# Eight key pages before the stream, a kept raw memory, and samples' outputs ahead of the diagonals in a two-layer decoder step

## The reference, cut to what matters

```python
def memory_kv(mem, g_mem, w_mem):                       # once for each layer
    k, v = jnp.split(rmsnorm(mem, g_mem) @ w_mem, 2, axis=-1)
def fox_layer(...):                                     # layer 0
    q, k, v, f, q_mem, gate = jnp.split(rmsnorm(x, g_pre) @ w_in, FOX_SPLITS, axis=-1)
    logf = log_sigmoid(f + b_f)
    o_tok = attend(q, k, v, logf)    # samples: k_pool[page_table], v_pool[page_table], decays
    o_mem = memory_attend(q_mem, mem_k, mem_v)
    y = (concat(o_tok, o_mem) * silu(gate)) @ w_o
    return x + rmsnorm(y, g_post)
def wkv_recurrence(...):                                # layer 1, per token
    sa = einsum('bhvk,bhk->bhv', S, -kk_t)
    S = S * w_t + sa[..., None] * (kk_t * a_t) + v_t[..., None] * k_t
    y_t = einsum('bhvk,bhk->bhv', S, r_t)
```

## Time and profile before

| | us |
|---|---|
| median of 3 runs | 1873.95 (1868.57 to 1874.59) |
| the profiled execution | 1869.83 |
| its span | 1868.1 |
| work outside the span | 1.7 |
| TensorE busy, weight loads busy | 1704.2, 1301.7 |
| VectorE busy | 964.6 |
| ScalarE busy | 378.3 |
| GpSimd busy | 161.2 |
| HBM traffic over the span | 226 GB/s |

### The profile page before, as it was taken

The page is one execution under the profiler, slowest core; times in us unless marked ns, Lnnn a source line. Parts: engine busy times, 40 slices in busy tenths (PEclk is TensorE's granted clock), DMA queues, the critical chain, the costliest instruction groups (busy, mean ns, idle before and its releaser), DMA issues.

```text
span 1868.1 us, 25962 instructions
## 1 busy us (share of the span) xinstructions
PE 1704.2 (91%) x8786; PEld 1301.7 (70%) x8786; DVE 964.6 (52%) x4842; ACT 378.3 (20%) x954; POOL 161.2 (9%) x295
## 2 busy tenths in 40 slices
PE   8999978898889998989979989999999998899996
PEld 6867755566566666657867767777777776678885
DVE  4346757655565655422352467776777776431103
ACT  2010112111121111211110323333333333121101
POOL 0001212122112222110000000000000000020000
PEclk9999989999989999999999999999999998999998
DMA  9239999999999999974353222222222214364331
GB/s 363 98 127 411 396 421 368 415 414 419 417 350 420 418 419 417 354 274 180 141 191 135 83 94 94 94 94 94 94 94 94 94 27 152 102 237 174 135 136 47
DMA packets 103637, 424.31 MB, mean 227 GB/s; under 512 B 42028, under 2 KB 48080, under 8 KB 93776
## 3 DMA queue, kind: packets, MB, share of 16 engines
q0 software_dynamic: 41680, 218.91, 29.4%
q1 hardware_dynamic: 53400, 189.64, 27.1%
q10 hardware_dynamic: 8424, 14.10, 2.0%
HBM read 409.74 MB, written 12.87 MB: 226 GB/s over the span
## 4 chain that ended last, share of the span: by engine, by line
PE 59%; DMA 23%; DVE 11%; issue 3%; SPq 2%; ACT 1%; POOLq 1%; POOL 0%; ACTq 0%; DVEq 0%
PE psum L683 12%; PE psum L631 10%; PE psum L620 10%; DMA kvr<-in_cv 9%; DMA kvr<-in_ck 9%; PE psum L983 7%; PE psum L857 3%; DVE kvr L1730 2%; SPq L512 2%; DVE kmT L2085 2%; PE psum L669 2%; DVE kmT L2083 2%; DMA kmT<-solved_t 1%; PE psum L1051 1%; PE psum L1069 1%
## 5 line engine op out<-in xcount | busy, mean ns | idle before, releaser
L1730 DVE CUSTOM_DVE_ANT_0 kvr<-kvr,arena 128x128 f32<-128x128 f32 x1536 | 334.5, 285 | 162.7 <-DMA kvr<-in_ck 162.6
L631 PE MATMUL psum<-hT,wring 128*128 128x264 f32 x1408 | 346.7, 402 | 0.0
L631 PEld LDWEIGHTS psum<-hT,wring 128*128 128x128 f32 x1408 | 270.6, 197 | 81.3 <-issue 31.0
L983 PE MATMUL psum<-hT,kvr 128*128 128x264 f32 x1152 | 292.7, 402 | 0.0
L983 PEld LDWEIGHTS psum<-hT,kvr 128*128 128x128 f32 x1152 | 221.4, 198 | 44.8 <-issue 6.4
L857 PE MATMUL psum<-kvr,arena 128*32 128x384 f32 x1024 | 116.0, 527 | 43.0 <-DMA kvr<-in_cv 40.0
L683 PE MATMUL psum<-hT,kvr 128*128 128x264 f32 x512 | 124.6, 400 | 1.3 <-DMA kvr<-in_wg 1.3
L1730 DVE DVE_READ_ACCUMULATOR2_ANT arena<- 128x1 f32 x1536 | 123.3, 80 | 0.0
L631 PE MATMUL psum<-gT,wring 128*128 128x256 f32 x512 | 120.1, 391 | 0.0
L620 PE MATMUL psum<-gT,wring 128*128 128x264 f32 x512 | 115.9, 390 | 0.8 <-DVE gT L1950 0.8
L631 PEld LDWEIGHTS psum<-gT,wring 128*128 128x128 f32 x512 | 97.8, 195 | 24.3 <-issue 10.7
(11 more groups left out here) (384 smaller groups left out, 1981.0 us busy)
## 6 DMA issues: line engine op xcount, KB each, us to landing
kvr<-in_ck POOLq DMA_DIRECT2D x128, 768.0 KB, 13.1
kvr<-in_cv POOLq DMA_DIRECT2D x128, 768.0 KB, 14.2
kvr<-in_wrkv SPq DMA_DIRECT2D x12, 3072.0 KB, 14.8
wring<-in_wkv SPq DMA_DIRECT2D x12, 2048.0 KB, 11.6
wring<-in_wm SPq DMA_DIRECT2D x8, 2048.0 KB, 12.0
wring<-in_wg SPq DMA_DIRECT2D x8, 2048.0 KB, 11.7
wring<-in_wo SPq DMA_DIRECT2D x8, 2048.0 KB, 8.2
kvr<-in_wg SPq DMA_DIRECT2D x8, 2048.0 KB, 9.8
```

Source lines behind the costliest of these rows:

```text
L631: last = mm(psum[:, m % 2, 0:n], w[:, k, t * P:(t + 1) * P], rhs[:, k, 0:n], start=(k == 0), stop=(k == KT - 1))
L983: last = mm(psum[:, m % 2, 0:T], w[:, k, t * P:(t + 1) * P], hT[:, k, :], start=(k == 0), stop=(k == KT - 1))
L1730: last = v_.tensor_tensor_reduce(page, page, qb[:, n % 2, h * P:(h + 1) * P], 1.0, 0.0, ALU.mult, ALU.add, S[:, n % 2, j * FH + h:j * FH + ...
```

## The change

1. **Eight key pages early.** `FIRST = KRING + VRING`: pages 0 to 3 go to the key ring and pages 4 to 7 to the value ring, all issued without a wait. The first four value pages are issued at slots 12, 14, 16 and 18. The scores of these eight pages are made in three chunks of four heads (`first_scores`), two of them on VectorE inside the prologue, the third in slots 0 to 7. To that end TensorE and ACT spread query chunks 0 and 1 inside the prologue (after units 2 and 4); chunk 2 stays where all three stood.
2. **The memory.** `memv` stays raw; layer 0's normed copy goes to `memv0` (in `oT`), and its 16 scaling instructions move from the prologue to slot 4 of VectorE's stream. The second load of the memory and its wait are gone.
3. **The plan.** Slots 0 to 7 weigh 0.4, slots 8 to 18 0.85, later ones 1.0 when the steps are spread.
4. **The turn.** On VectorE `diagonals()` moves behind the samples' outputs and the `prepared` increment.

```diff
--- before.py
+++ after.py
@@ -129,7 +129,9 @@
 NK = KST[-1]
 
 V_OVER = NK - KRING
-K_FILLS, V_FILLS = NK // KRING + 1, NK // VRING - 1
+K_FILLS, V_FILLS = NK // KRING, NK // VRING
+
+FIRST = KRING + VRING
 
 LAG = 3
 VSLOT = []
@@ -139,7 +141,7 @@
 SLOTS = VSLOT[-1] + 1
 V_AT = {slot: n for n, slot in enumerate(VSLOT)}
 
-V_EARLY = {6 + 3 * n: n for n in range(VRING)}
+V_EARLY = {FIRST + KRING + 2 * n: n for n in range(VRING)}
 STREAM_OF = [n for n in range(N_STREAMS) for _ in range(NPG[n])]
 
 NCH = [NS if x == MS else FH // 4 for x in STREAMS]
@@ -183,10 +185,13 @@
 
 def steps_of_slots():
 
+
+    weight = [0.4 if n < FIRST else 0.85 if n < VSLOT[0] else 1.0 for n in range(LAST_FILL)]
+    ends = [sum(weight[:n + 1]) / sum(weight) for n in range(LAST_FILL)]
     out, spent = [[] for _ in range(SLOTS)], 0.0
     for x in STEPS0:
         for part in [(*x, n) for n in range(4)] if x[0] == "unit" else [x]:
-            out[min(int(spent / TOTAL0 * LAST_FILL), SLOTS - 1)].append(part)
+            out[min(sum(e <= spent / TOTAL0 + 1e-9 for e in ends), SLOTS - 1)].append(part)
             spent += COST[x[0]] / (4 if x[0] == "unit" else 1)
     return out
 
@@ -403,6 +408,8 @@
         gmem = lambda l: gvec[:, 2, l, :]
         memv = gflat[:, 0:KT * NMEM].rearrange("p (k t) -> p k t", k=KT)
 
+        memv0 = oT[:, :, 0:NMEM]
+
         def val(i, per, k):
 
             return k if i is None else i * per + k
@@ -468,10 +475,6 @@
                     sp.dma_start(muL[:, :], I["muL"]).then_inc(sem("vec_in2"), 16)
                     sp.dma_start(lnv[:, :, :].rearrange("p a b -> p (a b)"), I["lnv"]).then_inc(sem("vec_in2"), 16)
                     sp.dma_start(shL[:, :, :], I["shL"]).then_inc(sem("vec_in2"), 16)
-                if (kind, first) == ("k", 0):
-
-                    sp.wait_ge(sem("p_done"), M_OF["m0", 7] + 1)
-                    sp.dma_start(gflat[:, 0:KT * NMEM], I["memT"].rearrange("p k t -> p (k t)")).then_inc(sem("mem_in2"), 16)
                 if (kind, first) == ("wo", 2):
 
                     sp.wait_ge(sem("u_out"), 1)
@@ -575,9 +578,10 @@
             for slot in range(SLOTS):
                 if slot < NK:
                     i = STREAM_OF[slot]
-                    if slot >= KRING:
-                        pool.wait_ge(sem("k_used"), slot - KRING + 1)
-                    page("k", kring, "k_full", slot, STREAMS[i], slot - KST[i])
+                    if slot >= FIRST:
+                        pool.wait_ge(sem("k_used"), slot - (FIRST if slot < FIRST + KRING else KRING) + 1)
+                    ring, full = (vring, "v_full") if KRING <= slot < FIRST else (kring, "k_full")
+                    page("k", ring, full, slot, STREAMS[i], slot - KST[i])
                 if slot in V_EARLY:
                     n = V_EARLY[slot]
                     page("v", vring, "v_full", n, STREAMS[STREAM_OF[n]], n - KST[STREAM_OF[n]])
@@ -768,7 +772,7 @@
                     if kind in ("m0", "m1"):
                         if at[1] == 0:
                             pe.wait_ge(sem("n_out"), 1 if kind == "m0" else 2)
-                        half_tile(m, half, memv, NMEM)
+                        half_tile(m, half, memv0 if kind == "m0" else memv, NMEM)
                     else:
                         half_tile(m, half, hT, T)
                 elif name == "f":
@@ -806,8 +810,10 @@
             def spread_queries(n, c):
                 x, nth = STREAMS[n], CST[n] + c
                 pe.wait_ge(sem("qb_c"), nth)
-                if nth == 0:
-                    pe.wait_ge(sem("lf_d"), 3)
+                if nth < 2:
+                    pe.wait_ge(sem("p_free"), M_OF["q", 4 * c + 3] + 1 + 2)
+                if nth:
+                    pe.wait_ge(*((sem("lf_c"), 1) if nth == 1 else (sem("lf_d"), 3)))
                 if x == MS and c == 0:
                     pe.wait_ge(sem("p_free"), M_OF["qm", 3] + 1 + 2)
                 for h in range(4):
@@ -836,7 +842,7 @@
                 x, j = STREAMS[n], v - KST[n]
                 ring = vring if v < V_OVER else kring
                 if v < V_OVER:
-                    pe.wait_ge(sem(f"v_full{v % VRING}"), 16 * (v // VRING + 1))
+                    pe.wait_ge(sem(f"v_full{v % VRING}"), 16 * (v // VRING + 2))
                 else:
                     pe.wait_ge(sem(f"k_full{v % KRING}"), 16 * K_FILLS)
                 if j == 0:
@@ -916,22 +922,26 @@
                     tile(2 * u, hT, T)
                     tile(2 * u + 1, hT, T)
                 if u == 2:
+                    spread_queries(0, 0)
                     sum_squares(1, oT, NMEM)
                     pe.wait_ge(sem("pt_in"), 48)
+                    pe.wait_ge(sem("qb_c"), 1)
                     for h in range(FH):
 
                         last = mm((Wp, Xp, Vp)[h // 4][:, h % 4 * P:(h % 4 + 1) * P], LF[:, h:PAGE_W:FH], cst[:, C_REV:C_REV + P],
                                   start=True, stop=True)
                     last.then_inc(sem("lf_t"), 1)
                 if u == 4:
+                    spread_queries(0, 1)
                     pe.wait_ge(sem("lf_fs"), 1)
-                    for c in range(3):
+                    for c in (1, 2, 0):
+                        if c == 0:
+                            pe.wait_ge(sem("qb_c"), 2)
                         out, cols = (Wp, Xp, Vp)[c], slice(c * 512, (c + 1) * 512)
                         mm(out, cst[:, C_TRI:C_TRI + P], lfT[:, cols], start=True, stop=False)
                         mm(out, ones, Fs[:, cols], start=False, stop=True).then_inc(sem("d_t"), 1)
             pe.wait_ge(sem("p_free"), M_OF["q", 11] + 1 + 2)
-            for c in range(FH // 4):
-                spread_queries(0, c)
+            spread_queries(0, 2)
             for slot in range(SLOTS):
                 done = V_ENDS.get(slot)
                 if done is not None:
@@ -1399,6 +1409,7 @@
             root(0, rs)
             for u in range(6):
                 if u == 2:
+                    queries_out(0, 0)
                     root(1, rsm)
                     act.wait_ge(sem("lf_t"), 1)
                     act.wait_ge(sem("n_ss"), 2)
@@ -1406,12 +1417,12 @@
                         last = ac(lfT[:, c * 512:(c + 1) * 512], (Wp, Xp, Vp)[c], ACT.Copy)
                     last.then_inc(sem("lf_c"), 1)
                 if u == 4:
-                    for c in range(3):
-                        act.wait_ge(sem("d_t"), c + 1)
+                    queries_out(0, 1)
+                    for nth, c in enumerate((1, 2, 0)):
+                        act.wait_ge(sem("d_t"), nth + 1)
                         ac(DS.rearrange("p (n h) -> p h n", h=FH)[:, 4 * c:4 * c + 4, :],
                            (Wp, Xp, Vp)[c].rearrange("p (h n) -> p h n", h=4), ACT.Copy).then_inc(sem("lf_d"), 1)
-            for c in range(FH // 4):
-                queries_out(0, c)
+            queries_out(0, 2)
             nth = 0
             for slot in range(SLOTS + 1):
                 if slot in V_ENDS:
@@ -1689,8 +1700,6 @@
                 elif name == "dm":
                     decays_of(at[0])
                 elif name == "mn":
-                    if at[0] == 0:
-                        dve.wait_ge(sem("mem_in2"), 16)
                     for k in range(4 * at[0], 4 * at[0] + 4):
                         last = stt(memv[:, k, :], memv[:, k, :], gmem(1)[:, k:k + 1], rsm, ALU.mult, ALU.mult)
                     if at[0] == 3:
@@ -1711,10 +1720,23 @@
                     tt(gT[:, 4 * c:4 * c + 4, 0:NPR], oT[:, 4 * c:4 * c + 4, 0:NPR], gT[:, 4 * c:4 * c + 4, 0:NPR],
                        ALU.mult).then_inc(sem("gp_out"), 1)
 
+            def first_scores(k, c):
+
+                if k == 0:
+                    dve.wait_ge(sem("qb_c"), c + 1)
+                if c == 0:
+                    dve.wait_ge(sem(f"k_full{k}" if k < KRING else f"v_full{k - KRING}"), 16)
+                for h in range(4 * c, 4 * c + 4):
+                    page = kvr[:, k * PAGE_W + h * P:k * PAGE_W + (h + 1) * P]
+                    last = v_.tensor_tensor_reduce(page, page, qb[:, 0, h * P:(h + 1) * P], 1.0, 0.0,
+                                                   ALU.mult, ALU.add, S[:, 0, k * FH + h:k * FH + h + 1])
+                return last
+
             def page_scores(k):
                 n = STREAM_OF[k]
                 x, j = STREAMS[n], k - KST[n]
-                dve.wait_ge(sem(f"k_full{k % KRING}"), 16 * (k // KRING + 1))
+                if k >= FIRST:
+                    dve.wait_ge(sem(f"k_full{k % KRING}"), 16 * (k // KRING))
                 if x == MS:
                     dve.wait_ge(sem("qb_c"), CST[n] + j + 1)
                     for t in range(2):
@@ -1725,10 +1747,12 @@
                 else:
                     if j == 0:
                         dve.wait_ge(sem("qb_c"), CST[n + 1])
-                    for h in range(FH):
+                    for h in range(FH if k >= FIRST else 0):
                         page = kring[:, k % KRING, h * P:(h + 1) * P]
```

(19 more changed lines are left out.)

## The result

| | us |
|---|---|
| median before, same chip (4 runs) | 1873.68 (1868.57 to 1874.59) |
| median of the changed kernel (4 runs) | 1827.64 (1826.47 to 1830.07) |
| ratio, with its 95% interval | 0.976 (0.974 to 0.978) |
| the profiled execution, its span | 1830.07, 1828.3 |

The changed kernel is 46.0 us faster; five more runs beside another set of the kernel before gave 1829.06 against 1870.33, 41.3 us. The forecast of 1834 is 6.4 us too high, inside its range. One run each of `turn_only` (4329.86 us) and of `gate_scale` (2182.72 us) fell in a much slower state, and every median in this document is over the other runs.

What follows compares the result with a forecast made beforehand. The stream was taken as bound by transfers until the key pages end, then by TensorE, the turns by a latency on the chain. 1869.8 - 29 (turns) - 8 (stream) = 1832.8, plus 1 for the median: 1834 us, range 1822 to 1856.

Steps and rivals of the forecast that it cites:

- The turn's mechanism: In the turns, samples' outputs run inside VectorE's 4.50 us wait for solved blocks, so `lora()` and the transposes start earlier.
- T+0.6: In the turn, predicted start of L1130 (L1140 after the change), 0.6 us behind T, the end of `diagonals`; 1.8 us earlier.
- The turn's sum: All passages between turns together: 29.1 us gained, taken as 29, with bounds 16 and 34.
- eight that read like rows 7: Eight of twelve turn passages, like the profiled one with transposes at T+15.70: 2.6 us each, 20.8 in all.
- The gate units' turn: Turn where the gate units begin and TensorE stands for the load of `in_wg`: a gain of 0.3 us.
- VectorE binds the turns: Rival for the turns: VectorE's list is as long as TensorE's, gain 1.33 us a turn, 16 in all; 1847 us, chance 0.17.
- The rival of the collision: Slower rival in the turns: SP's 3 MB load delays the solved blocks' read by x in 12 turns; 1894 us, chance 0.05.
- The stream: Transfer-bound stretch before the turns: 13.0 - 2.5 - 2.7 = 7.8 us gained, taken as 8, bounds 0 and 13.
- The 13 us of the bytes: In the stream, 5.25 MB moved early or no longer loaded, by 404 GB/s: 13.0 us gained.
- the rival that the stream keeps its length: Rival for the stream: fuller slots meet steps that already stall, early bytes are given back; 1842 us, chance 0.18.
- The 2.5 us for the gap before page 12: In the early stream, DMA stands some 2.5 us because page 12 is released only by slot 8; subtracted from the gain.
- The 2.7 us for fuller slots: In the stream's last 16 slots TensorE has no free time, 16 x 0.17 = 2.7 us subtracted from the gain.

Runs made afterwards that it cites:

- `turn_only`: Kernel before with only the turn's edit, `diagonals()` behind the samples' outputs and the `prepared` increment: 1843.66 us, ratio 0.985.
- `gate_scale`: `gate_early` with the memory's 16 scaling instructions at slot 12 instead of slot 4: 1821.31 us, ratio 0.976.
- `gate_early`: Changed kernel with the first of the gate units' loads issued one turn earlier: 1822.99 us, ratio 0.974.
- `turn_undone`: Changed kernel with `diagonals()` back ahead of the samples' outputs: 1849.27 us, ratio 0.989.
- `four_early`: Changed kernel with four key pages before the stream instead of eight: 1837.08 us, ratio 0.982.
- `reload`: Changed kernel with the memory's second load (2.1 MB) and VectorE's wait for it put back: 1833.70 us, ratio 0.980.
- `even_plan`: Changed kernel with all 144 slots weighing the same, as before the change: 1831.55 us, ratio 0.979.

## Why the prediction was right, point by point

**The turn's mechanism: right.** Each of its steps is in the trace: no wait of `lora()` behind the first passage, L1140 at T+0.53 for T+0.6, L1026 at T+12.95 as worked out, turns of 43.6 us for "some 44". The prediction's choice among 1.33, 1.8 and 2.75 us was 2.6; the clock stayed full in all nine regular passages, so it was 2.75. In the first it fell later on, behind a wait of 2.12 us (0.89 from 1082 to 1097 us). `turn_only` gives 28.2 us for the turn by itself, for the predicted 29.

**The turn's sum: 29 for 28.8, but by errors that cancel.** The table has 28.2 - 1.1 + 1.7 = 28.8 us. I had thirteen passages: the "eight that read like rows 7" included the first one, for which I added 1.5 us again. There are seven. From the traces: 7 x 2.75 (15.70 to 12.95) + 4.2 (17.18 to 12.95) + 1.3 (14.28 to 12.95) + 3.6 for the first (15.68 to 12.11) = 28.4, against 28.2 of the table. So seven times my 2.6, 18.2, should have stood where I wrote 20.8 (the traces give 19.3), the passage with L1016 at T+17.2 gave 4.2 for my 3.9, the first passage was mis-sized (1.5 for 3.6: before, its transposes came at T+15.68 too, a normed pair or not), the gate units' turn gained nothing where I had 0.3, and the last stretch gave 1.7 us with my 1.3 in it.

**The gate units' turn: wrong by its own argument.** I read that TensorE stands for `in_wg` and that the load follows from the end of the projections. That means that every microsecond TensorE gains ahead of it becomes waiting time. I wrote a small gain, 0.3 us; the traces show the wait grown from 1.29 to 4.81 us and a turn as long as before, within about a microsecond. `gate_early` shows the price of that wait: the turn is 6.2 us shorter in its trace, the medians 5 to 7.

**The rival "VectorE binds the turns": half true.** VectorE does bind them, by its list. But its sum of 16 us assumed that before the change VectorE bound them too. In nine of ten passages before, the clock fell and L1016 stood at T+15.68 or later, so the move gives 1.33 by the list and 1.4 by the clock. `turn_undone` separates the two: in five of its passages only the list is left to gain.

**The rival of the collision: not seen.** I had read rows 11 as if three loads would follow the read at once; only the smallest does, since the others have waits of their own. The price 12x was for x over 3.1 us; VectorE's idle time before `diagonals` fell by as much as was moved into it. The rule of the Trainium skill, "DMA: Bandwidth & Descriptors", section "Latency and other measured facts", of up to 2 us of HBM latency at high load, did not decide here; the traces don't show the read under the full load, as the 3 MB are issued 4 us behind it, and it has landed by then; `in_vrkv`, which does follow at once, costs it nothing.

**The stream: 8 for 12.4, one term with the wrong sign.** VectorE waits less for key pages, and TensorE is not near 100% in the middle, as foretold; the first value page is at 183.6 and not near 180. The 13 us of the bytes hold: `four_early` and `reload` measure them one by one, and with them the rival that the stream keeps its length falls. The 2.5 us for the gap before page 12 hold too, as far as can be seen: 351 GB/s for 404 over 20 us are 1.06 MB, 2.6 us, and `gate_scale`, which fills half of that, ends the stage 1.3 us earlier. The 2.7 us for fuller slots took the plan's cost and not its gain: `even_plan` is 2.5 to 4 us slower, so a gain of some 2 us stands where I subtracted 2.7. With it the stream is 13.0 - 2.5 + 2 = 12.5, and the forecast 1869.8 - 29 - 12.5 + 1 = 1829, for the measured 1827.64 and 1829.06. This fit is not proof of each term, for the stage is known no better than to some microseconds: the same old stream ended at 850.8 us in one trace and at 856.2 in `turn_only` (whose profiled execution lies 3.8 us over its median), so the stage's gain is 12 to 18 us by traces, and 22.6 - 7.8 (the clock in `turn_undone`'s turns) = 15 us by medians.

**Open.** Why the granted clock falls in one passage and not in another with the same idle time before it. Before, it fell in eight of nine regular passages, behind stretches without a matmul of 2.03 to 3.49 us; in `turn_undone` in four of nine; in the twelve kernels with the turn edit in four of 108, each behind 1.60 to 1.63 us, while 17 others of 1.50 to 2.06 us kept it. So short stretches go with the full clock, but the idle time isn't the whole of it. Also open is which part of the medians' 46.0 or 41.3 us beyond the spans' 39.8 belongs to which stage.

## What to carry to other kernels

Where an engine waits for a transfer and short work that needs nothing from it stands behind the wait, moving that work ahead gains its own length by the engine's list, and as much again where it ends an idle stretch that had lowered TensorE's clock; look at the duration of the same matmuls in other passages to see which you have. A wait for a load that isn't released earlier takes in all that the change gains ahead of it: find it in the same turn and issue the load earlier. A plan's weights move work, so both ends of the move belong in the sum. And a stage read from one trace is known only within its scatter, 4 us for this stream in seven traces: look at every kernel that has the stage unchanged before a microsecond of it is explained.

## What the runs showed of the hardware that I had not expected

- A semaphore increment written as an instruction of its own behind a VectorE operation is seen by TensorE while that operation runs: L1004 starts at 1209.25 us, `diagonals` runs from 1209.05 to 1210.27. So in this kernel it didn't hold TensorE until that operation's end.
- At equal idle time TensorE's clock fell or stayed: 2.03 us and 1.2 GHz before, 2.11 us and 2.4 GHz in `turn_undone`; 1.63 us and a fall in `gate_early`, 1.65 us and none in the changed kernel.
- Time gained early in the transfer-bound stream by another order, with no byte less, mostly doesn't reach its end: in `gate_scale` 4.4 us at the first value page became 1.3 us at the output projection and 0.8 in the median, about the 1.2 us that the fuller window (382 for 358 GB/s) is worth.
